# Second attention: the addition into the output stands behind the softplus and its split in VectorE's turn

## The reference, cut to what matters

```
z = einsum('bqhd,bkhd->bhqk', q, k) * B_DH ** -0.5
log_keep = where(valid, log_sigmoid(-z), 0)
after = cumsum(log_keep, axis=3, reverse=True) - log_keep
a = where(valid, exp(log_sigmoid(z) + after), 0)
o = einsum('bhqk,bkhd->bqhd', a, v)          # then * silu(g), @ w_out
```

## Time and profile before

| | us |
|---|---|
| median of 3 runs (2177.05 to 2178.77) | 2177.99 |
| the profiled execution's own time | 2175.86 |
| its span, first to last instruction | 2174.1 |
| TensorE busy in it (89%) | 1928.7 |
| VectorE busy (57%) | 1248.0 |
| ScalarE busy (47%) | 1021.1 |
| GpSimd busy (16%) | 342.9 |
| mean granted TensorE clock, share of 2.4 GHz | 0.942 |

### The profile page before, as it was taken

How to read it: one execution, slowest core, us unless ns; L and a number is a source line. 1 busy time by engine, 2 the same in 40 slices (tenths; PEclk the granted TensorE clock), 3 DMA queues, 4 the chain that set the end, 5 groups by cost and what they waited for, 6 DMA issues and landing times. The chain is left out here.

```text
span 2174.1 us, 35553 instructions
## 1 busy us (share of the span) xinstructions
PE 1928.7 (89%) x11420; PEld 1655.1 (76%) x11420; DVE 1248.0 (57%) x2633; ACT 1021.1 (47%) x2385; POOL 342.9 (16%) x561
## 2 busy tenths in 40 slices
PE   2989999899899599886699999999999999779996
PEld 2877878778778489886577777777777777579995
DVE  4455555465464522443277767676867677754455
ACT  4455454454454522444255555454545464532335
POOL 0111111111111000354011111110101111100241
PEclk7999999999999899998899999999999999879998
DMA  3112111112111242111111101010101011133213
GB/s 128 49 50 60 47 44 57 56 35 63 58 34 45 89 113 82 57 58 46 49 48 33 49 29 49 29 49 29 49 29 54 25 54 43 43 118 103 59 42 127
DMA packets 161890, 124.21 MB, mean 57 GB/s; under 512 B 11136, under 2 KB 152768, under 8 KB 161792
## 3 DMA queue, kind: packets, MB, share of 16 engines
q1 hardware_dynamic: 161792, 123.08, 18.7%
HBM read 89.53 MB, written 33.52 MB: 57 GB/s over the span
## 5 line engine op out<-in xcount | busy, mean ns | idle before, releaser
L105 PE MATMUL lb_pj<-lb_w_high,h_high 128*128 128x384 f32 (+1 forms) x576 | 208.4, 362 | 24.6 <-DVE lb_w_low L1280 15.0
L105 PE MATMUL la_pj<-la_w_high,h_high 128*128 128x384 f32 (+1 forms) x576 | 209.1, 363 | 11.7 <-DVE la_w_low L578 11.7
L105 PE MATMUL lb_pj<-lb_w_high,h_low 128*128 128x384 f32 (+1 forms) x576 | 199.7, 347 | 0.0
L105 PE MATMUL lb_pj<-lb_w_low,h_high 128*128 128x384 f32 (+1 forms) x576 | 198.7, 345 | 0.0
L105 PE MATMUL la_pj<-la_w_low,h_high 128*128 128x384 f32 (+1 forms) x576 | 196.6, 341 | 0.0
L105 PE MATMUL la_pj<-la_w_high,h_low 128*128 128x384 f32 (+1 forms) x576 | 196.2, 341 | 0.0
L1457 POOL TENSOR_TENSOR lb_o<-lb_o,lb_keep 128x512 f32<-128x512 f32 (+3 forms) x80 | 77.5, 969 | 623.4 <-ACT lb_keep L1161 623.4
L1137 ACT ACTIVATE lb_m<-lb_m 128x512 f32<-128x512 f32 (+4 forms) x200 | 98.7, 521 | 142.8 <-DVE lb_m L1301 140.9
L1301 DVE TENSOR_SCALAR lb_m<-lb_sc 128x512 f32<-128x512 f32 (+4 forms) x200 | 101.5, 547 | 66.2 <-PE lb_sc L1534 51.0
L1314 DVE TENSOR_TENSOR lb_s<-lb_sc,lb_m 128x512 f32<-128x512 f32 (+4 forms) x200 | 110.1, 551 | 46.8 <-ACT lb_m L1142 46.7
L105 PEld LDWEIGHTS lb_pj<-lb_w_high,h_high 128*128 128x128 f32 (+1 forms) x576 | 108.3, 188 | 35.1 <-issue 16.4
(11 more groups left out here) (296 smaller groups left out, 5264.3 us busy)
## 6 DMA issues: line engine op xcount, KB each, us to landing
stage<-in_a_w_in SPq DMA_DIRECT2D x60, 192.0 KB, 3.1
stage<-in_b_w_in SPq DMA_DIRECT2D x60, 192.0 KB, 2.6
stage<-in_ple_w_gate SPq DMA_DIRECT2D x22, 512.0 KB, 3.8
stage<-o_t SPq DMA_DIRECT2D x14, 528.0 KB, 3.7
mix_b_xs<-x_mid SPq DMA_DIRECT2D x8, 528.0 KB
norm_a_xt<-in_x SPq DMA_DIRECT2D x8, 512.0 KB, 3.6
stage<-in_a_w_in SPq DMA_DIRECT2D x16, 256.0 KB, 5.2
out_ak<-la_tok SPq DMA_DIRECT2D x8, 512.0 KB, 3.3
```

The lines of the kernel that those rows point to most:

```text
L105: last = pe.matmul(out, x, y, start=start and n == 0, stop=stop and n == 2, **kw)
```

## The change

Three places change the order of instructions; no instruction is added, removed or altered. In `stick_layer` VectorE's `finish(0)` and `add(i - 2)` move behind the softplus and split of pair i. In `mix_phase` ScalarE's `sigmoid(u)` moves ahead of `square(u - 1)` and `next_high(u - 1)`, and VectorE's `soft(u)` and `product(u)` move ahead of `next_low(u - 1)`. The last two stand under `not final`, so they reorder `mix_a` alone; `mix_b` gets the same order as before.

```
@@ stick_layer, vector, for i in range(NP + 1)
-                    if i - 2 == SAMPLE:
-                        finish(0)
-                    if i >= 2:
-                        add(i - 2)
                     if i < NP:
                         for s in units(i):
                             softplus(s)
                             if UNITS[s][0] < 2:
                                 split(s)
+                    if i - 2 == SAMPLE:
+                        finish(0)
+                    if i >= 2:
+                        add(i - 2)
@@ mix_phase, scalar
                         sigmoid_log(u)
+                        sigmoid(u)
                         if not final and u > 0:
                             square(u - 1)
                             next_high(u - 1)
-                        sigmoid(u)
@@ mix_phase, vector
                         clamp(u)
+                        soft(u)
+                        product(u)
                         if not final and u > 0:
                             next_low(u - 1)
-                        soft(u)
-                        product(u)
```

More of the change, by code:

```diff
@@ L1397, in body @@
                         gate_clamp(GATE_AT[i - 1])
[L1398 to L1401, removed]
                     if i < NP:
```

## The result

The changed kernel takes **2187.69 us** (median of 6 runs, 2186.74 to 2188.74) against 2178.5 of the kernel before in the same comparison (2177.05 to 2181.18): ratio 1.0041, interval 1.0029 to 1.0054. It is 9.2 us slower, where the forecast said 2178 and gave "slower" 0.29. The time lies 0.3 us inside the upper end of the range (2167 to 2188); the point was missed by 9.7 us.

A forecast was written before the change was run, and what follows sets the result against it. TensorE, busy 1928.7 of 2174.1 us, was taken as the bound. mix_a -19.8, stick_layer +17.9 and clock +2 sum to +0.1 us, giving 2178 against the median of 2177.99; range 2167 to 2188.

The forecast's parts named there:

- Where the change counts: TensorE's product waits in mix_a, 17.0 us; in stick_layer, additions free in 80 of 104 pairs while VectorE awaits the log.
- stick_layer, steps 4 to 8: Fourth group: scores(7) 0.54 us later, values(5) +1.7, values(6) +1.7 to +2.0; from step 8 nothing more lost.
- Last group: stick_layer's last group, VectorE-bound: 0.6 us in step 6, 0.73 in step 7, 0.15 a step, 0.7 at hand-over; +2.6.
- Clock in stick_layer: Half clock behind the new values(5) wait, bounded between nothing and 24 us over seven groups; taken as +2.
- the sign that the prediction had named for being wrong: stick_layer's granted clock clearly under that of before; listed among the signs that would show the forecast wrong.
- The first rival: Steps 7 and 8 of stick_layer: new waits lower the clock, 1.7 us in six groups, 10 us: 2188; chance 0.17.
- the others run at TensorE's pace: mix_a blocks outside the four that still load weights take TensorE's 14.7 us for three units.
- 1.0 for the square and high part that now stand ahead of the weight split: Item of mix_a's store loop: 1.0 us of ScalarE work ahead of its weight split.
- the loop of the four blocks that a store holds: mix_a, weight split to GpSimd's whole and back: 15.4 to 15.9 us a block against 14.7, some 0.9 each.
- The tail wait: End of mix_a's gate stage, 8.20 us wait for the sums: last unit's product 1.8 us earlier relative to TensorE's end.
- The second rival: mix_a's gain stays about 10 us because GpSimd, late by the store, holds clamp and next_low: 2188; chance 0.10.

The follow-up runs named there:

- run 1: Kernel before with only stick_layer's additions and finish(0) reordered, mix_a in its old order: 2200.39 us, ratio 1.0119.
- run 5: Kernel before plus 12 matmuls of 352 columns ahead of step 9's projection in seven stick_layer groups, no addition moved: 2194.55 us, ratio 1.0072.
- run 8: Kernel before plus 6 matmuls in each of three idle TensorE stretches at the head of a stick_layer group: 2167.28 us, ratio 0.995.
- run 9: Changed kernel plus 6 matmuls in each of three idle stretches at the head of a stick_layer group: 2177.23 us, ratio to before 0.9995.
- Run 11: Kernel before with only VectorE's new order in mix_a; ScalarE and stick_layer keep the old one: 2158.7 us, ratio 0.9908.
- run 12: Kernel before with VectorE's new order in mix_a and idle stretches filled at heads and ahead of scores(6), scores(7), except last group: 2139.38 us, ratio 0.9838.
- run 2: Kernel before with only mix_a reordered, on ScalarE and VectorE; stick_layer in its old order: 2162.2 us, ratio 0.9942.
- run 10: Kernel before plus 6 matmuls ahead of scores(6) and 12 ahead of scores(7) of stick_layer, seven groups: 2171.81 us, ratio 0.9966.
- run 7: mix_a reordered, stick_layer old; GpSimd's x1 sum in mix_a cut to 8 columns from the fourth gate unit on: 2159.32 us, ratio 0.9911.

## Where the prediction held and where it failed, step by step

The range held by 0.3 us, the sum did not: +0.1 was put down, and the spans differ by 11.0. That the time lies inside is in part luck. The upper end, 2188, is what each of two rivals gave when it took its full 10 us alone; both came true by about half, 5.6 us in mix_a and 4.7 at the heads, and no error went the other way to speak of.

**Where the change counts: right.** The additions were free where they stood. VectorE's idle time ahead of the softplus went to 98.6 us (about 90 expected), and the waits it caused stand at L1586 and L1592, where they were put.

**stick_layer, steps 4 to 8: right.** scores(7) was to be 0.54 late. It is 0.22 late behind the anchor, and the anchor itself stands 0.3 later by the addition of step 4. values(5) is 1.4 late in the fourth group (1.7), values(6) 1.7 to 1.9 in the six like groups (1.7 to 2.0), both behind the anchor. Nothing more is lost from step 8 to 13. Over seven groups this term is 15.4, worked out as 15.3, but the first group has 4.3 of it instead of 3.3, and the 0.3 of each group ahead of the anchor, 2.0 in all, stand among the +1.3 elsewhere. The groups last 108.7 to 109.2 us, without the last of the seven, for some 108 forecast.

**Last group: right in size, wrong in kind.** +2.9 for +2.6. But there values waits 1.1 to 2.6 us for the addition in each step from 7 on (9.4 us at L1371), where the text had 0.15 a step; most of that takes the place of other waits. values(6) stands 3.2 us late there and the last values 4.0, of which mix_b's first matmul wins back 1.1; that the sum fits is luck. Alone in run 1 it is +4.2.

**Clock in stick_layer: the term that was mis-sized, and put in the wrong place.** The text looked at steps 6 to 8 and took +2 there. In those steps nothing changed in six groups (3.4 us in both); the first group went from none to 3.4, which a profile can show without the change (run 5). The 4.7 us are lost at the next group's head, some 50 us behind values(6), by three waits that had been there all along. Over the seven groups the granted clock is 0.94, before it was 0.96: the sign that the prediction had named for being wrong. The first rival had the mechanism (half clock, some 10 us) at steps 7 and 8; run 5 showed that a longer group is enough, runs 8 and 9 that the small waits are what the clock falls on. Why a longer group makes such a head dearer is open. The Trainium skill (TensorE: Matmul & The Clock Gate, section "A second HAM failure mode: psum-queue depth-cycling") has short idle stretches between matmul groups make the clock go back and forth; the trace agrees, with three of 0.93 to 0.96 us within 5 us.

**mix_a: the step that failed is "the others run at TensorE's pace", together with "1.0 for the square and high part that now stand ahead of the weight split".** That 1.0 us was put into the loop of the four blocks that a store holds and left out of the others, where it stands too, because the first unit's clamp is queued behind VectorE's weight split, and that behind ScalarE's. Nor did the text see that next_low, now behind the product, meets GpSimd's addition of that product. The three other blocks were 16.15, 16.94 and 13.89, together 2.9 us over three times 14.7. Run 11, without ScalarE's edit, has them at 14.92, 14.57 and 13.30, and a gain of 18.7 of the 19.8 forecast; the edit itself costs 4.3 us of stage time (121.9 - 117.6). The four held blocks took 1.5, 1.0, 1.7 and 2.0 us over 14.7, where 0.9 each was put: 2.6 us more, another term mis-sized (its own items add up to 15.4 to 15.7 us a block, not to 15.9). The tail wait fell by 1.2, not 1.8. The second rival (mix_a's gain about 10, since GpSimd is late by the store) had the direction; the four blocks that it speaks of have 2.6 us of the 5.6 missing.

**The rest.** 1.3 us behind stick_layer and -0.4 ahead of mix_a are within what single profiles differ by; no run looks at them. What was not tried: the order of ScalarE alone, since with VectorE's old order each of the two engines would wait for the other.

## What to carry to other kernels

Before an instruction is moved out of a stretch where its engine idles, write down who is queued behind its new place; here that gave the loss at values(6) to 0.3 us in six of seven groups. When two engines are reordered for one chain, price each edit by itself: VectorE's was worth 19 us and ScalarE's took 4 to 6 of them back. And where TensorE is the bound, look for short waits whose stretch runs at half clock: filling them with matmuls whose result nobody reads gave 10 us at one place, 3 to 6 at another, and with both filled and VectorE's order together 36.

## What the runs showed of the hardware

Idle stretches of 0.93 to 0.96 us on TensorE, three of them within 5 us, took the granted clock from 2.4 to 1.2 GHz behind them, and filling them kept it at 2.4 (runs 8, 9 and 12). What such a place costs is not fixed: 1.7 us in one group and 3.4 in another, with the same instructions and nearly the same waits. Groups that were 1.9 us longer had 3.4 in five of six (run 5), but run 2 has it in three of six without a longer group ahead of the first of them, so no run shows all that decides. Taking the fall out of one place (run 10) brought 1.7 us more half clock at the next in five of six heads. A time lost to half clock at one place can therefore not be read off the edit at that place.

A VectorE subtraction of 128x256 with both inputs in SBUF took 0.42 us alone and 1.23 beside GpSimd's sum of 128x384, which took 1.99 instead of 1.02 (run 7 and the earlier trace rows against the changed kernel). next_low of 128x288 took 0.51 us when it started 0.23 ahead of GpSimd's addition and 1.27 when it started 0.06 behind it.
